# A hybrid attention and gMLP layer on eight cores: P*V of a step issued one step later behind its neighbour's scores, one score pass per single-key-block step, rotary tables on VectorE, a new drain

## The reference, cut to what matters

```python
h = rms_norm(x, norm_g) * (1 + scale) + shift          # scale, shift, gate = silu(c) @ w_ada + b_ada
z = h @ w_in                                           # (B, 2048, 8704)
for g, (window, dilation) in enumerate(((128, 1), (512, 4), (2048, 16))):
    q = partial_rope(rms_norm(qkv[:, :, g, 0], q_norm_g[g]), positions)   # 8 heads of 64
    k = partial_rope(rms_norm(qkv[:, :, g, 1], k_norm_g[g]), positions)
    o, lse = dilated_window_attention(q, k, qkv[:, :, g, 2], window, dilation)   # causal
attn = sum over g of softmax_over_g(lse) * o
y_a  = attn * silu(z_gateA)
u, v = split(gelu(z_B));  v = layer_norm(v)
y_b  = u * (W_s v + b) * silu(z_gateB)                 # W_s: causal 128x128 mixing per channel group
merged = sigmoid(mA) * (y_a @ w_branch_a) + sigmoid(mB) * (y_b @ w_branch_b)
out  = x + gate * (merged @ w_out)
```

## Time and profile before

| what | value |
|---|---|
| median of the runs (lowest) | 833.12 us (832.8) |
| profiled execution | 832.86 us; span of its slowest core 831.2 us |
| span of the 8 cores | 827.2 to 831.2 us |
| PE / DVE / ACT / POOL busy in the span | 91% / 57% / 46% / 32% |

### The profile page before, as it was taken

The page is one execution under the profiler, slowest core; times in us unless marked ns, Lnnn a source line. Parts: engine busy times, 40 slices in busy tenths (PEclk is TensorE's granted clock), DMA queues, the critical chain, the costliest instruction groups (busy, mean ns, idle before and its releaser), DMA issues.

```text
span 831.2 us, 14846 instructions; the slowest of 8 cores (827.2 to 831.2 us)
## 1 busy us (share of the span) xinstructions
PE 760.5 (91%) x4936; PEld 362.8 (44%) x4936; DVE 471.3 (57%) x739; ACT 379.2 (46%) x678; POOL 267.5 (32%) x356
## 2 busy tenths in 40 slices
PE   4578797989999999999999999889998999999994
PEld 0123453545655555444444444334443444444442
DVE  5535587865667777766777755766654233323332
ACT  3204686768775656666666742723221111111110
POOL 0401222232324433323222200366833333333343
PEclk9698899999999999999999999989999999999998
DMA  8991121242365000300000050619495122232223
GB/s 253 288 227 51 52 78 39 52 65 39 49 106 52 13 2 2 51 2 1 1 2 1 15 89 1 102 25 140 78 255 138 51 58 95 53 100 57 97 55 148
DMA packets 23482, 61.99 MB, mean 75 GB/s; under 512 B 5616, under 2 KB 12016, under 8 KB 20976
## 3 DMA queue, kind: packets, MB, share of 16 engines
q0 software_dynamic: 13472, 22.40, 18.2%
q1 hardware_dynamic: 7488, 30.26, 12.1%
q10 hardware_dynamic: 2448, 8.39, 2.5%
HBM read 75.05 MB, written 8.39 MB: 100 GB/s over the span
## 4 chain that ended last, share of the span: by engine, by line
PE 76%; DVE 11%; ACT 5%; issue 4%; DMA 1%; POOL 1%; DVEq 0%; ACTq 0%; POOLq 0%
PE ps L236 63%; DVE arena L245 11%; ACT arena L245 5%; PE ps L368 3%; PE ps L573 3%; PE ps L534 2%; PE ps L505 2%; PE ps L577 1%; POOL arena L245 1%; PE ps L344 1%; DMA arena<-wsp 1%; PE ps L847 0%; DMA arena<-misc 0%; DMA out<-arena 0%; DVEq L994 0%
## 5 line engine op out<-in xcount | busy, mean ns | idle before, releaser
L236 PE MATMUL ps<-arena 128*128 128x512 bf16 x2692 | 623.8, 386 | 15.3 <-DVE arena L245 12.2
L236 PEld LDWEIGHTS ps<-arena 128*128 128x128 bf16 x2692 | 276.9, 108 | 306.9 <-issue 38.7
L245 POOL TENSOR_TENSOR arena<-arena 128x128 bf16<-128x128 f32 (+4 forms) x322 | 247.7, 779 | 464.3 <-DVE arena L245 443.6
L245 ACT ACTIVATE arena<-ps 128x512 bf16<-128x512 f32 (+2 forms) x304 | 195.2, 671 | 326.5 <-PE ps L236 248.9
L245 DVE TENSOR_TENSOR arena<-ps,arena 128x512 f32<-128x512 f32 (+2 forms) x218 | 150.6, 733 | 86.8 <-PE ps L236 30.7
L245 DVE SCALAR_TENSOR_TENSOR arena<-arena,ps 128x512 f32<-128x512 f32 x80 | 54.4, 685 | 119.1 <-PE ps L236 101.3
L245 DVE TENSOR_REDUCE arena<-arena 128x8 f32<-128x512 bf16 x96 | 65.7, 684 | 76.1 <-ACT arena L245 76.0
L245 ACT ACTIVATE arena<-arena 128x16 f32<-128x16 f32 (+5 forms) x183 | 77.0, 427 | 43.3 <-DVE arena L245 32.7
L245 DVE TENSOR_TENSOR arena<-arena 128x1024 bf16<-128x1024 bf16 (+5 forms) x125 | 71.9, 577 | 21.5 <-ACT arena L245 19.9
L245 ACT ACTIVATE arena<-ps,arena 128x512 bf16<-128x512 bf16 x96 | 60.8, 685 | 16.1 <-PE ps L505 16.1
L245 DVE TENSOR_SCALAR arena<-arena 128x256 bf16<-128x256 bf16 (+6 forms) x84 | 56.4, 712 | 20.2 <-ACT arena L245 13.1
(11 more groups left out here) (36 smaller groups left out, 145.4 us busy)
## 6 DMA issues: line engine op xcount, KB each, us to landing
arena<-x SPq DMA_DIRECT2D x32, 512.0 KB, 5.4
arena<-w_in POOLq DMA_DIRECT2D x16, 1024.0 KB, 15.0
out<-arena ACTq DMA_DIRECT2D x15, 512.0 KB, 5.5
arena<-w_ada SPq DMA_DIRECT2D x7, 1024.0 KB, 18.2
arena<-w_adag SPq DMA_DIRECT2D x8, 512.0 KB, 8.8
arena<-w_out POOLq DMA_DIRECT2D x2, 1024.0 KB, 29.6
arena<-w_ada SPq DMA_DIRECT2D x2, 512.0 KB, 32.8
arena<-w_in POOLq DMA_DIRECT2D x4, 256.0 KB, 8.6
```

The costliest lines, as they stand in the source:

```text
L236: ins = e.matmul(out_ap, l, r, start=(i == 0), stop=(i == n - 1))
L245: P.op(eng, lambda e: getattr(e, meth)(*a, **kw), reads=reads, writes=writes)
```

## The change: what it does

1. **P*V a step later, both halves together.** `pv(c_,0)` and `pv(c_,1)` of step `it-4` stand right behind `scores(it-3, 1)`; `mask` of half 1 and `accum` move behind `rope`. The PE order becomes: proj 0, scores of half 0, (x transposes), proj 1, scores of half 1, pv of both halves, proj 2, transp. A fourth pT buffer lies in `qn[3]`.
2. **One score pass for one key block.** Such a step does the scores of all 8 heads at the place of half 1, with one Exp of 128x1024 and one mask instead of two of 128x512; `scores(it-3, 0)` is left out.
3. **Rotary tables on VectorE**: 12 multiplications of 128x256 instead of 24 of 128x128 on POOL, in three groups among the x_in and ada calls.
4. **x tiles a step earlier**: transposes of tile it+5, Square of it+7, load of it+10, `x_mod(it+4,2)` in iterations 4, 6, 8 and 10; ws4 and ws5 are loaded in iteration 10 instead of 11.
5. **finA an iteration later**, between `mask` of half 0 and the second sumsq; finB stays where it was.
6. **A drain written out by hand**: the loop ends at 47; finZ, V1, scores and pv are interleaved, the finB of tb = 3 stand ahead of V1(12) to V1(15), and V1(t) for t >= 8 uses banks 0, 1, 6, 7.
7. **The last output tile** has a key for each half, and each half's DMA its own.

```diff
-        for g in (1, 2, 0):
+        def rot_tables(g):
             for ro in range(2):
                 gi = 2 * g + ro
...
-                for hf in range(2):
-                    gv = grp[:, g, ro, 8 * hf:8 * hf + 8].unsqueeze(1).to_broadcast([128, 16, 8])
-                    X("pool", "tensor_tensor", ["cosT", "misc", "hd"], ["T1_%d" % g], out=T1[:, gi, :, 8 * hf:8 * hf + 8], in0=cg, in1=gv, op=ALU.mult)
-                    X("pool", "tensor_tensor", ["sinT", "misc", "hd"], ["T2_%d" % g], out=T2[:, gi, :, 8 * hf:8 * hf + 8], in0=sg, in1=gv, op=ALU.mult)
+                gv = grp[:, g, ro, :].rearrange("p (u d) -> p u d", u=2).unsqueeze(1).to_broadcast([128, 16, 2, 8])
+                for T_, tab, nm in ((T1, cosT, "cosT"), (T2, sinT, "sinT")):
+                    X("dve", "tensor_tensor", [nm, "misc", "hd"], ["T%d_%d" % (1 if T_ is T1 else 2, g)],
...
         x_in(3, 6)
+        rot_tables(1)
         ada_tr(0)
         ada_row(2)
         ada_col(1)
+        rot_tables(2)
         ada_tr(1)
         ada_row(3)
         ada_col(2)
+        rot_tables(0)
         ada_tr(2)
...
+            i = pt_new(s, h)
+            if nk == 1:
+                pt_of[(s, 1 - h)] = i
+            X("act", "activation", [B(SB[0]), B(SB[1])], ptk(i),
+              out=pT[i].rearrange("p e a k q -> p e (a k q)"), in_=ps[:, SB[0]:SB[0] + 2, :], func=AF.Exp, scale=0.125)
...
-            b = t % 2
+            b = (0, 1, 6, 7)[t % 4] if t >= 8 else t % 2
...
+        for it in range(4, NS):
+            a, b_, c_ = it - 1, it - 3, it - 4
+            xp = it + 7 if it + 7 < NT else None
+            proj(it, 0)
+            sumsq(it, 0)
+            if not one(b_):
                 scores(b_, 0)
                 mask(b_, 0)
+            if it - 1 in fin_at:
+                finA(*fin_at[it - 1])
+            if it + 5 < NT:
+                x_transp(it + 5, TB)
+                x_evac(it + 5, TB)
             if sc_x:
                 sc_x()
...
+            proj(it, 1)
+            sumsq(it, 1)
             if it - 1 in fin_at:
                 finB(*fin_at[it - 1])
+            scores(b_, 1)
+            pv(c_, 0)
+            pv(c_, 1)
+            rstd(it, 17 if xp else 16)
+            scaleqk(it, 0)
+            scaleqk(it, 1)
+            rope(it)
+            mask(b_, 1)
+            accum(c_, 0)
+            accum(c_, 1)
+            if it in (4, 6, 8, 10):
+                x_mod(it + 4, 2)
+            proj(it, 2)
+            vevac(it)
+            transp(a)
             if it in fin_at:
                 finZ(*fin_at[it])
-                finA(*fin_at[it])
...
+        scores(45, 0)
+        mask(45, 0)
+        finA(0, 2)
+        V1(0)
+        scores(45, 1)
+        pv(44, 0)
+        pv(44, 1)
+        mask(45, 1)
+        finB(0, 2)
+        finZ(1, 2)
+        accum(44, 0)
+        accum(44, 1)
+        transp(47)
+        V1(1)
...
+        finZ(3, 2)
+        accum(46, 0)
+        accum(46, 1)
+        V1(5)
+        sv_const()
+        finA(3, 2)
+        pv(47, 0)
+        pv(47, 1)
+        finB(3, 2)
+        V1(6)
+        accum(47, 0)
+        accum(47, 1)
+        finZ(0, 3)
+        V1(7)
...
+        V1(11)
+        finB(3, 3)
+        for t in range(12, 16):
+            V1(t)
...
-            X("dve", "tensor_tensor", [B(b), "gbc"], ["ot%d" % s], out=ot[s][:, hs], in0=banks[b], in1=gate_bc[:, hs], op=ALU.mult)
+            sk = "ot%d" % s if not last else "otl%d" % hf
+            X("dve", "tensor_tensor", [B(b), "gbc"], [sk] + (["ot%d" % s] if last and hf == 0 else []), out=ot[s][:, hs], in0=banks[b], in1=gate_bc[:, hs], op=ALU.mult)
...
-                     reads=["ot%d" % s], writes=["osb%d" % s], slot="osb%d%s" % (s, "_%d" % hf if last else ""))
+                     reads=[sk], writes=["osb%d%d" % (s, hf)], slot="osb%d%s" % (s, "_%d" % hf if last else ""))
```

More of the change, by code:

```diff
@@ L520, in kblocks, with ptk, pt_new, one @@
             return ([prev[s]] if prev[s] is not None else []) + [s]
+        def ptk(i):
+            return ["pT%d" % i] + (["qn30", "qn31"] if i == 3 else [])
+        def pt_new(s, h):
+            i = pt_i[0] % (4 if s > 3 else 3)
+            pt_i[0] = i + 1
+            pt_of[(s, h)] = i
+            return i
+        def one(s):
+            return len(kblocks(s)) == 1
         def scores(s, h):
@@ L524, in scores @@
             nk = len(kb)
[L525 to L526 removed]
+            cols = [(2 * h + a, ki_, k_, 128 * (a * 2 + ki_)) for a in range(2) for ki_, k_ in enumerate(kb)] if nk == 2 else \
+                [(c_, 0, s, 128 * c_) for c_ in range(4)]
             def fn(e):
                 ins = None
[L530 to L535 removed]
+                for c_, ki_, k_, o_ in cols:
+                    for e_ in range(2):
+                        rows = slice(64 * e_, 64 * e_ + 64)
+                        ins = e.matmul(banks[SB[e_]][:, o_:o_ + 128], kr[k_ % NK][rows, c_, :], qr[s % NQ][rows, c_, :],
+                                       start=True, stop=True)
@@ L579, in fn @@
                 return ins
-            P.op("pe", fn, reads=["pT%d" % i] + ["vr%d" % (k_ % NV) for k_ in kb], writes=[B(PB[h])])
+            P.op("pe", fn, reads=ptk(i) + ["vr%d" % (k_ % NV) for k_ in kb], writes=[B(PB[h])])
         def accum(s, h):
@@ L679, in build_nc @@
         x_mod(4, 4)
-        scores(0, 0)
-        mask(0, 0)
         transp(1)
@@ L779, in build_nc @@
                 load_w(1, OFF_GATE_B)
-            if 48 <= it < 51:
-                V1(4 * (it - 48) + 3)
-            if it == 51:
-                for t in range(12, 16):
-                    V1(t)
-                    finZ(t - 12, 3)
-                for hp in range(4):
-                    finA(hp, 3)
-                for hp in range(4):
-                    finB(hp, 3)
-            if it == 49:
-                sv_const()
+        scores(45, 0)
[12 more added lines that the diff above has]
+        V1(1)
+        scores(46, 0)
+        mask(46, 0)
+        finA(1, 2)
+        V1(2)
+        scores(46, 1)
+        pv(45, 0)
+        pv(45, 1)
+        mask(46, 1)
+        finB(1, 2)
+        finZ(2, 2)
+        accum(45, 0)
+        accum(45, 1)
+        V1(3)
+        scores(47, 0)
+        mask(47, 0)
+        finA(2, 2)
+        V1(4)
+        scores(47, 1)
+        pv(46, 0)
+        pv(46, 1)
+        mask(47, 1)
+        finB(2, 2)
+        finZ(3, 2)
[12 more added lines that the diff above has]
+        V1(7)
+        finZ(1, 3)
+        finA(0, 3)
+        V1(8)
+        finZ(2, 3)
+        finA(1, 3)
+        finZ(3, 3)
+        finB(0, 3)
+        V1(9)
+        finA(2, 3)
+        finB(1, 3)
+        V1(10)
+        finA(3, 3)
+        finB(2, 3)
+        V1(11)
+        finB(3, 3)
+        for t in range(12, 16):
+            V1(t)
         o_ring = off_ring
```

103 lines of the change are left out of this document (23 added, 80 removed).

## The result

The changed kernel takes 810.66 us (median of 10 runs, 809.62 to 811.31) against 833.17 (median of 20); the ratio is 0.9732, 95% interval 0.9723 to 0.9741. Eight of the 20 runs of the kernel before were slow ones (855 to 917 us), which the ratio leaves out. The forecast was 809.5 us. That these errors nearly cancelled is luck.

What follows compares the result with a forecast made beforehand. TensorE was taken as the bound, with 76% of the chain; -7.4 - 7.0 - 11.1 + 4.7 - 0.1 - 2.7 = -23.6 took 832.86 to 809.2, median 809.5 us. Forecast range 803 to 816 (chance 0.62), overall range 797 to 824.

Steps and rivals of the forecast that it cites:

- Tables, -7.4: Start: without POOL's 24 products, weight row 1 starts near 23 and the first projection comes at about 53.8 us; -7.4 us.
- x tiles, -7.0: x stage: waits of 3.29 and 3.01 us at steps 8 and 12 go, partly offset by late scaleqk; -7.0 us.
- The lag behind each modulation: x stage: scaleqk of the next step comes 1.7 to 2.1 us later than TensorE wants, four times; +7.6 us.
- P*V and one pass, -11.1: Steps with two and one key blocks: fewer boundaries -4.1, shorter one-key-block steps -7.6, iteration 24 0.6 more; together -11.1 us.
- The boundary from scores to P*V: TensorE's change from scores to P*V, not in the trace: counted as 0.11 us; if free, at most 4.8 us gained.
- Mask beside rope, charged nothing: Half-1 mask now beside rope: rope might end up to 0.7 us a step later; nothing charged.
- finA, +4.7: Fin iterations: late finA delays V's copy, finZ waits about 1.6 us, 10.8 us per iteration for 10.14; +4.7 us.
- Drain and UG, -0.1: Drain +1.6 us, and the 1.66 us wait at the first UG blocks goes; together -0.1 us.
- Last tile, -2.7: End: the second half's product no longer waits for the first half's output DMA; -2.7 us.
- finA harmless: Rival, fin iterations: nothing slides, the finA term is -3.3 and the time 801.5 us; chance 0.14.
- The gains went missing: Rival: start and x-stage gains missing, 824 us, or boundary costs stay, 820.6 us; chance 0.19.
- The falling clock in the fin iterations: Rival: finZ waits lower the clock, 3 to 7 us slower per fin iteration, middle 849.5 us; chance 0.05.

Runs made afterwards that it cites:

- both experiments: Against the changed kernel, finA put back right behind its finZ: 801.85 us; or finA left late and finB moved just ahead of finZ: 804.0 us.
- the experiment: Changed kernel with the last output tile's two halves sharing one name again: 814.5 us, 0.9769 of the kernel before.
- the first experiment: Changed kernel with the rotary tables back on POOL as 24 products at the start: 816.98 us, 0.9813 of the kernel before.

## Why the prediction was right, and where it was not

**Tables, -7.4, measured -5.25.** The mechanism held, and the landing of row 2's data too (35.23 against an estimate of 34.1). Mis-sized: row 2 was taken at 7.03 us and took 8.72 behind its wait, at a granted clock of 0.51 for 3.4 us of it. Row 1 took 8.06 for 9.4, but that only lengthened the wait for row 2's data. The products lay in VectorE's waits, as forecast, at 0.35 us each for 0.4.

**x tiles, -7.0, measured -10.67 in the loop and +1.41 ahead of it.** The removed waits were right. The lag behind each modulation was counted as 1.7 to 2.1, four times 1.9; the rows show 1.33, 1.39, 1.01 and 0.17, 3.9 in place of 7.6. With 3.9 the prediction's sum gives -10.7, what the stage shows. The modulation was taken at its old 3.18 us: behind mask and accum it takes 2.46, 0.7 less each time. Not foreseen was ScalarE's queue ahead of the loop, with 3.04 us at 95.50: the change puts tile 8's and 9's preparation ahead of V's copy there, and the edit that moved tile 8's part a projection earlier won 2.7 us up to step 13.

**P*V and one pass, -11.1, measured -6.14.** The two-key-block steps were right (-2.17 - 1.26 over nine steps, 0.38 each, for 0.41), and the boundary's 0.11 was borne out by parting P*V (0.35 for three). The boundary from scores to P*V, open in the prediction, costs what the others do: in step 39 P*V starts 0.33 us behind the start of the scores (365.09 to 365.42), a projection 0.32 to 0.33 behind it (362.93 to 363.25, in step 40 372.69 to 373.02). The one-key-block step was taken at 6.83 to 6.86 and is 6.96: 17 x 0.1 are 1.7 us. Iteration 24 was counted as 0.6 more; it cost 1.28 more of wait (2.05, where the trace of before has 0.77 there) and 1.64 of slow matmuls (5.29 for 3.65), 2.3 beyond. Step 12 with its 0.4 lies in the x stage by the table's cuts. The last 0.6 is not assigned.

**Mask beside rope, charged nothing.** Nothing waits for rope except in iteration 24, so the charge was right; the size of the delay was not. Rope is neither unchanged nor later by a whole mask of 0.7: its four operations take 2.8 to 2.9 us where they took 2.49. In 42 of the 48 steps rope starts 0.23 to 0.24 us behind the mask, when about 0.45 us of the mask are left, and its first product takes 0.97 to 0.99 us where it took 0.66 to 0.69. The Trainium skill (SBUF — State Buffer, Who interferes with whom) has the later instruction wait for the earlier one. The trace agrees, but what is left of the mask when rope starts is the most that this can cost, not the whole mask; 0.32 us were measured.

**finA, +4.7, measured +6.95.** The mechanism is confirmed by both experiments, and the wait was 1.56 for 1.6. The period was 10.95 for 10.8, seven times, and 11.21 once. The gain of 0.5 in iteration 39 did not come: in the kernel before no P*V waits in that iteration (389.02 follows the transposes at once), and the new finZ waits 0.38 us, so it lost 0.2.

**Drain and UG, -0.1, measured -3.7.** The drain cost 0.69 for 1.6. In UG, besides the 1.66, two waits of 0.85 and 0.97 at the spatial products went (another grew by 0.41), and a slow block of 64 matmuls took 15.67 for 16.50; the prediction looked at the first wait only. No experiment undoes the new drain, so its part is read from the rows alone, and why those waits went stays open.

**Last tile, -2.7, measured -3.73.** The size was right where the mechanism lies: the last product comes 14.08 us behind the start of the last output groups in place of 16.90, 2.8 less, and the experiment gives the wait as 2.99. The other 0.9 us lie behind the last product (7.02 for 7.93), where the last output lands. Over the eight cores that stretch took 6.9 to 8.4 us before and 7.0 in the changed kernel, but 7.0 to 8.5 in the kernel with two score passes, so it varies and is not shown to be a gain of the change.

**The rivals.** finA harmless: no; with finA put back the time was 801.85, near the 801.5 given for that case. The gains went missing only in parts. The falling clock in the fin iterations did not come:

```profile
376.00:462.00 86.00, 73.24 (x634) 1.00 0.00 1
```

Columns: stretch, its length, TensorE busy, granted clock, DMA share, GB/s. The eight waits of 1.56 to 1.82 left the clock at full level throughout.

## What to carry to other kernels

When work is moved a step later, list what stands behind it on the queue of every engine that it uses, and look for the short evacuation that frees a bank: here two operations of 1.35 us together, ahead of a 0.57 us copy, cost TensorE 1.2 us per iteration (10.95 against 9.77), and moving finA or finB away won them back. A delay also lengthens the life of buffers: with eight V buffers, P*V a step later was possible only ahead of the copy that reuses V's ring. And price a moved operation by who runs beside it in its new place, not by its old row.

## What the runs showed of the hardware

VectorE and POOL hold each other up, and the rows show by how much. In the kernel before, an operation of the modulation that started 0.01 us behind a product of rope (at 156.73, 0.66 us) took 0.73 us, until that product was over; beside no product it takes 0.33:

```profile
156.74 0.73 DVE L245 TENSOR_SCALAR arena<-arena 128x256 bf16<-128x256 bf16 x1
```

In the changed kernel rope starts 0.23 us behind the mask at 122.17, and it is rope's first product that takes longer:

```profile
122.40 0.98 POOL L245 TENSOR_TENSOR arena<-arena 128x256 f32<-128x256 bf16 x1 [4.62 <-DVE arena L245]
```

So the pairing decides who pays: rope takes 2.8 to 2.9 us for 2.49, while the modulation, which used to start with rope and took 3.15 to 3.18, now starts when about half of rope is done and takes 2.46 to 2.49. Products on end are worse: a scaling that started 0.84 us into POOL's run of 24 took 9.02 us (9.23 in the first experiment) in place of 0.75 and ended only behind the run (30.50 for 29.94).

The length of a wait does not tell by itself whether the clock falls behind it. In the changed kernel's iteration 24, four cores waited 2.04 to 2.05 us and their next 16 matmuls took 5.1 to 5.3 us (granted clock 0.50, the 1.2 GHz level):

```profile
274.70:278.10 3.40, 3.40 (x11) 0.50 0.00 0
```

The other four waited 0.99 to 1.22 us and stayed at 3.62. Yet in the kernel with tile 8 prepared early the same wait of 2.04 left the group at 3.63, and in the changed kernel's UG a wait of 2.23 at 538.03 was followed by 64 matmuls at full pace (13.99), one of 2.02 at 556.50 by 15.67. What else decides stays open.
